# Two modulation sums and their transfers moved, and a new instruction order in the recurrent stage

## The reference

```python
mod = c_act @ ada_w[layer] + ada_b[layer]
shift, scale, gate = jnp.split(mod, 3, axis=-1)
h = rmsnorm(x, norm_g[layer]) * (1.0 + scale[:, None, :]) + shift[:, None, :]
...
xr, gate = proj[..., :LRU_WIDTH], proj[..., LRU_WIDTH:]      # xr is convolved to xc
r = jax.nn.sigmoid(xblk @ w_a + b_a)                         # by blocks of 128 columns
i = jax.nn.sigmoid(xblk @ w_x + b_x)
log_a = -LRU_C * r * jax.nn.softplus(-lam)
u = jnp.sqrt(-jnp.expm1(2.0 * log_a)) * (i * xc)
state = exp(log_a) * state + u                               # a scan over the 256 tokens
y = (states * jax.nn.silu(gate)) @ w_out
...
x = x + gate[:, None, :] * y
```

## Time and profile before

| what | value |
|---|---|
| median of 3 runs | 907.64 us (906.79 to 909.63) |
| the profiled execution's own time | 908.5 us |
| its span | 906.7 us |
| TensorE busy | 851.8 us, 94% |
| VectorE busy | 719.2 us, 79% |
| ScalarE busy | 507.0 us, 56% |
| mean granted TensorE clock | 0.985 |

### The profile page before, as it was taken

The page is one execution under the profiler, slowest core; times in us unless marked ns, Lnnn a source line. Parts: engine busy times, 40 slices in busy tenths (PEclk is TensorE's granted clock), DMA queues, the critical chain, the costliest instruction groups (busy, mean ns, idle before and its releaser), DMA issues.

```text
span 906.7 us, 14872 instructions
## 1 busy us (share of the span) xinstructions
PE 851.8 (94%) x5722; PEld 774.9 (85%) x5722; DVE 719.2 (79%) x1138; ACT 507.0 (56%) x877; POOL 76.7 (8%) x121
## 2 busy tenths in 40 slices
PE   3899899999999999999999999999899999999976
PEld 3767689999999989999798889999779899889964
DVE  4776888878878878889888788686778766789996
ACT  2226657455345465568473445544475768756992
POOL 2110100010000000132000022010000000000000
PEclk9999899999999999999999999999999999999998
DMA  9997774788887748986847789987535784446621
GB/s 319 366 314 268 255 253 142 234 279 284 304 317 276 258 161 293 381 323 201 310 164 253 275 249 284 273 238 248 180 118 164 244 278 164 136 156 224 217 93 47
DMA packets 124998, 216.31 MB, mean 239 GB/s; under 512 B 12507, under 2 KB 98247, under 8 KB 118784
## 3 DMA queue, kind: packets, MB, share of 16 engines
q1 hardware_dynamic: 108156, 133.48, 44.4%
q0 software_dynamic: 13808, 73.51, 23.3%
q10 hardware_dynamic: 2964, 8.37, 2.7%
HBM read 214.18 MB, written 1.15 MB: 237 GB/s over the span
## 4 chain that ended last, share of the span: by engine, by line
PE 57%; DVE 20%; ACT 10%; DMA 7%; issue 5%; SPq 0%; POOL 0%; DVEq 0%; ACTq 0%
PE bank L586 9%; PE bank L588 9%; PE bank L587 9%; PE bank L592 6%; PE bank L594 6%; PE bank L593 6%; DVE w_lo L1759 5%; DMA modraw<-in_mod_w 4%; DVE modsum L1791 3%; ACT w_hi L1199 2%; DVE of L1791 2%; PE bank L691 2%; DMA vv<-in_mod_w 1%; ACT kk L1261 1%; DMA raw<-in_moba_w_in 1%
## 5 line engine op out<-in xcount | busy, mean ns | idle before, releaser
L1759 DVE TENSOR_TENSOR w_lo<-raw,w_hi 128x1024 fp32r<-128x1024 f32 (+1 forms) x236 | 276.1, 1205 | 65.5 <-ACT w_hi L1199 64.9
L586 PE MATMUL bank<-h_hi,w_hi 128*128 128x256 f32 x1072 | 306.5, 286 | 5.3 <-DVE w_lo L1759 4.0
L588 PE MATMUL bank<-h_hi,w_lo 128*128 128x256 f32 x1072 | 303.2, 283 | 0.0
L587 PE MATMUL bank<-h_lo,w_hi 128*128 128x256 f32 x1072 | 303.2, 283 | 0.0
L1199 ACT ACTIVATE w_hi<-raw 128x1024 fp32r<-128x1024 f32 (+1 forms) x236 | 237.4, 1038 | 65.7 <-DMA raw<-in_moba_w_in 20.1
L586 PEld LDWEIGHTS bank<-h_hi,w_hi 128*128 128x128 f32 x1072 | 205.5, 192 | 7.9 <-issue 5.2
L587 PEld LDWEIGHTS bank<-h_lo,w_hi 128*128 128x128 f32 x1072 | 205.6, 192 | 1.3 <-issue 0.5
L588 PEld LDWEIGHTS bank<-h_hi,w_lo 128*128 128x128 f32 x1072 | 205.5, 192 | 0.0
L592 PE MATMUL bank<-w_hi,o_hi 128*128 128x512 f32 x304 | 122.4, 403 | 6.7 <-ACT w_hi L1199 3.3
L594 PE MATMUL bank<-w_hi,o_lo 128*128 128x512 f32 x304 | 119.3, 392 | 0.0
L593 PE MATMUL bank<-w_lo,o_hi 128*128 128x512 f32 x304 | 119.0, 392 | 0.0
(11 more groups left out here) (322 smaller groups left out, 1261.6 us busy)
## 6 DMA issues: line engine op xcount, KB each, us to landing
raw<-in_ffn_w_in SPq DMA_DIRECT2D x88, 512.0 KB, 6.6
modraw<-in_mod_w POOLq DMA_DIRECT2D x32, 1024.0 KB, 6.9
raw<-in_ffn_w_out SPq DMA_DIRECT2D x44, 512.0 KB, 7.6
modraw<-in_ada_w POOLq DMA_DIRECT2D x16, 1024.0 KB, 5.4
raw<-in_attn_w_in SPq DMA_DIRECT2D x26, 512.0 KB, 5.4
raw<-in_moba_w_in SPq DMA_DIRECT2D x24, 512.0 KB, 9.3
modraw<-in_mod_w POOLq DMA_DIRECT2D x20, 512.0 KB, 4.6
modraw<-in_ada_w POOLq DMA_DIRECT2D x16, 512.0 KB, 4.8
```

The lines of the kernel that those rows point to most:

```text
L586: pe.matmul(dst, cut(hi(u)), a_hi, start=first, stop=False, skip_group_check=True)
L587: pe.matmul(dst, cut(hi(u)), a_lo, start=False, stop=False, skip_group_check=True)
L588: return pe.matmul(dst, cut(lo(u)), a_hi, start=False, stop=last, skip_group_check=True)
L1759: dve.tensor_tensor(lo(v), raw_unit(v), hi(v).bitcast(F32), ALU.subtract).then_inc(sem("w_lo_ready"), 1)
```

## The change

It does four things. The last group of modulation blocks gets four half places, so that its transfers can be issued further ahead. Two more of its sums are made in `after_attention`, and the `modulate(2)` at the end of the recurrent stage goes. On VectorE `scans` is split into `scan_input` and the scans proper, and `rates(1)` stands between them; `ratio(1)`, `o_low`, and the low parts of weight units stand in another order. On ScalarE `decay_tanh(1)` comes ahead of the two gate sigmoids, and two conversions of weight units come later.

```diff
-    halved = range(2 * KT, 3 * KT)
+    halved = [*range(2 * KT, 3 * KT), *range(len(mods) - KT, len(mods))]
...
             gates_out(1, unit0("wax", 1) + AHEAD)
+            decay_tanh(1)
             gate_sigmoid(0)
             gate_sigmoid(1)
-            ahead(unit0("l_gate", 2) + AHEAD)
-            decay_tanh(1)
+            ahead(unit0("l_gate", 2) + AHEAD - 1)
             decay_exp(1, 0)
             gated_high(0)
             decay_exp(1, 1)
+            ahead(unit0("l_gate", 2) + AHEAD)
             gated_high(1)
-            ahead(unit0("l_gate", 2) + 1 + AHEAD)
             sqrt_table()
             input_root(1)
             gate_out(2)
...
             def after_attention(i):
                 if i >= 2:
-                    modulate(1)
+                    modulate(2)
...
-            def scans(i):
+            def scan_input(i):
                 a, b = 4 * i, 4 * i + 4
                 dve.wait_ge(sem("input_root"), i + 1)
                 dve.wait_ge(sem("ix_ready"), i + 1)
                 link(dve.tensor_tensor(tiles(vv, a, b), tiles(vv, a, b), tiles(of, a, b), ALU.mult))
-                for n in range(a, b):
+
+            def scans(i):
+                for n in range(4 * i, 4 * i + 4):
                     dve.tensor_tensor_scan(tiles(bias, n, n + 1), tiles(qz, n, n + 1), tiles(vv, n, n + 1), 0.0,
                                            ALU.mult, ALU.add).then_inc(sem("scanned"), 1)
...
             gated_input(0)
+            scan_input(0)
+            rates(1)
             scans(0)
-            rates(1)
             ahead(unit0("l_gate", 3) + 1)
             opened(0)
             gated_rows(0)
             ahead(unit0("lru_o", 0))
             opened(1)
+            o_low(kk, 0, 20)
             gated_rows(1)
-            o_low(kk, 0, 20)
+            ratio(1)
             ahead(unit0("lru_o", 0) + 1)
             gated_input(1)
-            ratio(1)
             o_low(kk, 1, 20)
-            ahead(unit0("lru_o", 1))
+            ahead(unit0("lru_o", 1) + 1)
+            scan_input(1)
             scans(1)
-            ahead(unit0("lru_o", 1) + 1)
             for m in (2, 3):
                 gated_rows(m)
+            ahead(unit0("lru_o", 2))
             for m in (2, 3):
                 o_low(kk, m, 20)
-            modulate(2)
             out_projection("lru_o", lambda i: fold(10, (0, 1)) if i == 2 else None)
```

## The result

The changed kernel took 910.60 us (median of 20 runs, 906.78 to 913.07) against 907.96 us of the kernel before (20 runs). The ratio is 1.0034 with a 95% interval of 1.0021 to 1.0048. That is 3.1 us slower (1.9 to 4.4), where +1.3 us was forecast; the two medians alone differ by 2.6 us. The median lies inside the stated range, but "no change", which had most of the chance, is not what came: the kernel is slower, by somewhere between 0.21% and 0.48%.

What follows compares the result with a forecast made beforehand. TensorE was taken to bound most of the kernel, VectorE its part near the end. +2.6 us at the attention end and −1.3 at row 4 gave +1.3, so 908.9 us; 8 in 10 within 905.7 to 910.9.

Steps and rivals of the forecast that it cites:

- no change: Whole kernel: a time that cannot be told from before, within 0.3% or 2.7 us; chance 0.73.
- The sum: Whole kernel: +2.6 us at the end of attention and −1.3 us at row 4 give +1.3 us.
- The sums at the end of attention: In `after_attention`: four sums instead of two delay all that follows by 2.6 us, bounds 0 and 2.7.
- the clock falls at the norm after attention: Rival, norm after attention: TensorE waits bring half clock, costing up to 1.7 us, total up to +3.0; chance 0.16.
- Part 2, rates and tanh first: Ahead of the first scans and gates: tanh does not wait, the low part stays at 863.35; no gain by itself.
- Part 3, the waits for u2 and u3: Recurrent stage: VectorE waits for ScalarE's high parts, from 872.9 to 873.4 for u2 and 1.7 us for u3.
- Row 4's idle time: Last product: TensorE stands idle before row 4 for 4.0 us, against 3.34 before.
- The gain of 1.3 us at row 4: Last product: row 4 starts at about 884.2 against 885.48, a gain of 1.3 us.
- half clock again at the same price: Last product: half clock follows row 4's wait as before, with 6.17 us for row 4 and the fold.
- The signs: Prediction wrong if `block_sum` 3 starts before 810, second scans under 4 us later than 875.5, or clock falls between 808 and 830.
- The third sign: Around the norm after attention: prediction wrong if granted clock falls between 808 and 830.
- The table load: ScalarE, path to u3: 1.29 us per load by the trace, not 2.66 by the skill page, which would give about +4.1.

Runs made afterwards that it cites:

- e2: The kernel before with only the four half places, four sums in `after_attention` and no `modulate(2)` at the end; ratio 1.0006 to the kernel before.
- e4: The changed kernel with the low part of the weight unit u3 back behind the second scans; ratio 1.0006 to the kernel before.
- e6: The changed kernel with 24 idle TensorE products between rows 3 and 4 of `lru_o`; ratio 1.0025 to the kernel before.
- e12: The kernel before again, no edit; one execution for its profile, no ratio.
- e7: The changed kernel with 17 and 9 idle TensorE products instead of 5 and 5 in two waits of the norm after attention; ratio 0.9998 to the kernel before.
- e9: The kernel before with four half places and the last two sums moved ahead of `rates(0)` and `branch(2)`; ratio 0.9965 to the kernel before.
- e10: The changed kernel with the last two sums ahead of `rates(0)` and `branch(2)`, and u3's low part behind the second scans; ratio 0.9967 to the kernel before.
- e11: The kernel before with the edits of e2 and e7 together; ratio 0.9989 to the kernel before.
- e1: The changed kernel timed again, no edit, six runs; ratio 1.0059 to the kernel before.
- e13: The changed kernel timed a third time, no edit, twelve runs; ratio 1.0029 to the kernel before.
- e3: The changed kernel without the sums' move, only the new order kept; ratio 1.0000 to the kernel before.
- e8: The changed kernel with two sums in `after_attention` and one each ahead of the low parts of u2 and u3; ratio 0.9979 to the kernel before.

## Why the prediction was wrong

**The step that failed is TensorE's clock, in two terms.** The sum put it at nothing at the norm, and it took the same price for it before and after at row 4. The moves of VectorE's work came out nearly as forecast.

**The sums at the end of attention: right, and their second price was missed.** "Cost: +2.6 us" was measured as 2.8, just above the stated bound of 2.7: a pair of sums was priced by the 2.59 us to the next instruction, and each further sum in a row takes 1.39. The prediction then let the delay pass through the norm unchanged. In three profiles of the changed kernel, and in those of e2, e4 and e6, which have the same waits at the norm, the clock fell four times out of six, and B was 6.05 to 6.16 us instead of 4.80: 1.3 us. In all eight profiles in which these waits are filled or never arose, B is 4.79 or 4.80. **This is the first term that failed**: the rival "the clock falls at the norm after attention" had a chance of 0.16 and no part in the sum, and it came in four of six profiled executions. Against it the prediction said "these are two short pieces, and 1.51 and 1.40 us had no such effect". Here 1.73 to 1.77 us and about 0.67 us, with five short products between them, had one. The length of the waits does not tell the executions apart: the changed kernel's first profile and e4 kept full clock behind 1.76 and 0.67 us. What does was not found out.

**Part 2, rates and tanh first: right.** ScalarE's tanh follows its sigmoids without a wait, and the low part behind scans and rates starts 9.39 us after `ratio(0)`, where it was 9.37.

**Part 3, the waits for u2 and u3: right.** 0.5 and 1.7 us were forecast and 0.53 and 1.63 came. Row 4's idle time was forecast as 4.0 us and is 3.57.

**The gain of 1.3 us at row 4: right for the start of the row, about nothing at the end of the product.** Row 4 starts 30.15 to 30.17 us after `ratio(0)` in all three profiles of the changed kernel and 31.50 in the kernel before, which is the forecast gain. The prediction then said "I take half clock again at the same price". **This is the second term that failed.** From row 4 to the last product the kernel before takes 14.12 us in one execution and 12.55 in the other, and the changed kernel 14.13, 15.18 and 15.14. The first value of each is nearly the same, so the two first profiles bear the prediction out: D fell by 1.34 us. Over all of them D is 44.8 on average before and 45.0 in the changed kernel, so the gain is about nothing: an estimate from two and three profiles, no more. Where the clock stays full in both, D falls from 44.06 to 43.24 (e12, e7): 0.8 us, as the product then takes 13.09 us from row 4 on instead of 12.55; 0.32 us of that is a wait of TensorE for the low parts of u5 to u7.

**The sum.** +2.8 at the sums, +0.9 at the norm (1.3 us in four of six) and +0.3 in C (means of 85.3 before and 85.6) give +4.0 us, an estimate from these profiles. The measured +3.1 (1.9 to 4.4) holds it. It would also hold +2.8 and +0.3 without the norm, so the median by itself does not show the norm's share; B in the profiles does, and with less certainty e7 against the changed kernel. Worked out in the same way, against the mean C of 85.3, e7 comes to +0.5 (measured −0.2), e9 to −3.4 (−3.2), e10 to −3.3 (−3.0) and e11 to −1.3 (−1.0). How often the clock falls at the norm is known only from those six profiles.

**The signs.** `block_sum` 3 and the second scans came as late as forecast. The third sign, a granted clock that falls between 808 and 830, was missing in the first profile and is there in e1 and e13.

**The table load.** The row of the changed kernel says 1.28 us from 879.00, the conversion ahead of it ends at 878.98, and the silu starts at 880.29. So there is no further time on either side of it, and going by the row was right.

**Smaller slips.** A row of 12 products takes 2.82 us by its two starts (869.33 to 872.15), not 2.72, which is 12 at 0.227 without the longer start. Nothing in the sum hangs on it.

**What the change wanted was right.** Taking the sums from in front of the last weight units is worth about 3 us (e9, e10). It was spent again by putting them where VectorE was just as late, and by asking for u3 ahead of the scans.

## What to carry to other kernels

Work that is taken off one critical place has to go where the engine waits today; the trace lists these places as idle times with a releaser, and two waits of 1.04 and 0.76 us took two sums of 1.28 us at no cost, where a gapless stretch charged 2.8 us for two. Before asking for an operand earlier, look at what stands in front of its producer: moving one low part ahead of the scans made VectorE wait 1.63 us for a conversion behind a table load. A delay of one engine is also idle time of TensorE, and its price includes the clock: where filler products cover a wait, their number has to grow with the wait.

## What was not expected of the hardware

Two short waits of TensorE close together were followed by half clock: 1.73 to 1.77 and about 0.67 us with five short products (0.85 us) between them, in four of six profiles. A wait of 3.34 to 3.60 us before row 4 was followed by a full row at half clock (e1, e13), by a part of one (before, changed, e3), or by none (e7, e12); 3.18 us in e8 were followed by half clock too. The same kernel did both, behind 3.34 and 3.35 us. So one profile does not price a clock fall.
